# Two choices at once on four 64x64 quarters of the array, tile by tile, in a two-layer routed-expert kernel

## The reference, cut to what matters

```python
q = (xt @ w_query).reshape(n, 8, 2, 128)          # 16 units of 128 columns
s = einsum('nhpd,pkd->nhpk', q, subkeys)           # scores of 128 keys, twice a head
s1, i1 = top_k(s[:, :, 0], 16); s2, i2 = top_k(s[:, :, 1], 16)
best, ic = top_k(all sums s1 + s2, 16)             # 16 experts for each of 8 heads
expert, gate = i1[...] * 128 + i2[...], softmax(best)
act = gelu(einsum('nd,nhkd->nhk', xt, w_up[expert])) * gate
y = einsum('nhk,nhkd->nd', act, w_down[expert])    # 128 choices a token
```

## Time and profile before

| | before |
|---|---|
| device time, median of 3 runs (lowest, highest) | 5051.02 us (5049.02, 5064.87) |
| span of the profiled execution | 5042.8 us |
| PE matmul busy | 4367.6 us (87%) |
| DVE busy | 3163.9 us (63%) |
| ACT busy | 1188.3 us (24%) |
| POOL busy | 1621.6 us (32%) |
| moved by DMA | 1472.42 MB, mean 292 GB/s |
| choices' gathers (queue q0, with some other loads) | 1263.35 MB |

### The profile page before, as it was taken

How to read it: one execution, slowest core, us unless ns; L and a number is a source line. 1 busy time by engine, 2 the same in 40 slices (tenths; PEclk the granted TensorE clock), 3 DMA queues, 4 the chain that set the end, 5 groups by cost and what they waited for, 6 DMA issues and landing times. The chain is left out here.

```text
span 5042.8 us, 49934 instructions
## 1 busy us (share of the span) xinstructions
PE 4367.6 (87%) x17024; PEld 2583.3 (51%) x17024; DVE 3163.9 (63%) x7441; ACT 1188.3 (24%) x2971; POOL 1621.6 (32%) x1418
## 2 busy tenths in 40 slices
PE   8899999999989877789999897799999987777555
PEld 6866677755444323334476776776544443232111
DVE  6523323247878789855556644432778788995776
ACT  2211211113323323221111223110333232332111
POOL 0412000014444444433330241100444444444554
PEclk9999999999999999999999999999999999999777
DMA  2223232329999999999993234441999999999998
GB/s 110 84 74 120 73 127 96 137 115 415 415 409 410 416 420 413 412 420 419 419 419 149 84 109 166 169 163 40 387 419 404 412 413 420 420 413 418 416 414 342
DMA packets 266368, 1472.42 MB, mean 292 GB/s; under 512 B 27009, under 2 KB 77953, under 8 KB 113601
## 3 DMA queue, kind: packets, MB, share of 16 engines
q0 software_dynamic: 176608, 1263.35, 61.4%
q1 hardware_dynamic: 79168, 198.75, 10.7%
q10 hardware_dynamic: 10336, 7.12, 0.5%
HBM read 1433.90 MB, written 55.34 MB: 295 GB/s over the span
## 5 line engine op out<-in xcount | busy, mean ns | idle before, releaser
L3036 PE MATMUL ps<-early,diag 128*128 128x512 f32 (+1 forms) x3464 | 1692.2, 634 | 416.8 <-ACT diag L2944 416.3
L2826 POOL DMA_INDIRECT early<-in_peer,ids x980 | 1148.4, 1172 | 1430.1 <-PE ps L3036 1257.6
L2868 DVE SCALAR_TENSOR_TENSOR early<-early,rows 128x1024 f32<-128x1024 f32 x980 | 1184.2, 1223 | 443.9 <-DMA early<-in_peer,ids 441.8
L3036 PEld LDWEIGHTS ps<-early,diag 128*128 128x128 f32 (+1 forms) x3464 | 647.8, 195 | 1370.6 <-ACT diag L2944 679.0
L2944 ACT ACTIVATE diag<-consts_sb,weight 128x128 f32<-128x128 f32 (+1 forms) x1010 | 354.3, 391 | 769.5 <-DVE weight L2880 754.0
L1335 PE MATMUL ps<-hT,gate_ring 128*128 128x288 f32 (+2 forms) x1728 | 465.0, 424 | 6.4 <-ACT gate_out L1347 3.4
L1335 PEld LDWEIGHTS ps<-hT,gate_ring 128*128 128x128 f32 x1728 | 319.7, 193 | 144.9 <-issue 34.6
L2933 ACT ACTIVATE gel<-dot 128x2 f32<-128x2 f32 x576 | 117.4, 204 | 1116.3 <-DVE early L2868 925.0
L3036 PE MATMUL ps<-late,diag 128*128 128x512 f32 (+1 forms) x432 | 228.5, 671 | 83.5 <-ACT diag L2944 82.7
L2966 PE MATMUL ps<-late 128*128 128x320 f32 (+2 forms) x1024 | 251.8, 399 | 0.0
L2826 POOL DMA_INDIRECT late<-in_peer,ids x136 | 164.6, 1211 | 199.2 <-PE ps L3036 163.5
(11 more groups left out here) (394 smaller groups left out, 5859.3 us busy)
## 6 DMA issues: line engine op xcount, KB each, us to landing
gate_ring<-in_in_gate POOLq DMA_DIRECT2D x48, 512.0 KB, 4.2
slot<-in_w_branch SPq DMA_DIRECT2D x16, 1152.0 KB, 5.2
ring<-in_in_delta SPq DMA_DIRECT2D x8, 2048.0 KB, 8.4
late<-in_peer_query SPq DMA_DIRECT2D x32, 512.0 KB, 7.9
early<-in_peer,ids POOLq DMA_INDIRECT x980, 15.5
slot<-gate_rows SPq DMA_DIRECT2D x16, 864.0 KB, 7.0
slot<-in_in_pool SPq DMA_DIRECT2D x6, 2048.0 KB, 10.7
gate_ring<-in_in_gate SPq DMA_DIRECT2D x24, 512.0 KB, 10.8
```

What stands on the lines that cost most here:

```text
L2826: pool.indirect_dma_start(place(q), None, table_rows, bass.IndirectOffsetOnAxis(ap=ids[:, n, c:c + 1], axis=0)).then_inc(s.pair[PLACE[q]], 16)
L2868: nc.vector.scalar_tensor_tensor(out=up, in0=up, scalar=1.0, in1=rows[:, n, :], op0=ALU.mult, op1=ALU.mult, accum_out=dot[:, i % 2, k:k + ...
L3036: ins = nc.tensor.matmul(g.ps[0:r, 2 * (n % 2) + m, :], diag[:, (SUMMED[q] - 1) % DIAGS, 0:r], place(q)[:, D + m * 512:D + (m + 1) * 512], ...
```

## The change

All tiles go in turn. PE takes a group's two choices at once: the array is used as four quarters of 64 rows and 64 columns, for each half of the tokens (r) and each choice of the group (k). Choice k of half r is summed in PSUM partitions 64k to 64k+63, banks 2r and 2r+1. So a group is 8 matmul calls of 64x64 by 512 columns where it was 4 of 128x128. `x` is no longer added by PE nor copied by ACT: DVE adds the two choices' sums to it at the start of the next tile (`fold`), during which PE waits. DVE adds no choices of its own. Places come free by groups. Four more heads' halves are asked for ahead of group 0, the routes of tiles 0 and 1 are in one stretch of 60 groups, and the projections' units come one in each group, from group 209 on. The ring of 10 places ends at choice 32 and returns at choice 114.

```diff
-TOGETHER = 2
-HEADS = [(n, h) for h in range(PH) for n in range(TOGETHER)] + [(n, h) for n in range(TOGETHER, TILES) for h in range(PH)]
+HEADS = [(n, h) for n in range(TILES) for h in range(PH)]
+BY_GROUP = [(n, c) for n in range(TILES) for c in range(0, COUNT[n], GROUP)]
 ROUTE_AT = {}
 for _h in range(PH):
+    for _at, _head in ({0: (0, _h + 1), 4: (1, _h)} if _h < PH - 1 else {0: (1, _h)}).items():
+        ROUTE_AT.update({_h * STEP + _at + k: _head + (k,) for k in range(4)})
+for _i, _head in enumerate(itertools.product(range(2, TILES), range(PH), range(4))):
+    ROUTE_AT[PH * STEP + _i] = _head
...
-EXTENDED = 244
+EXTENDED = 114
-ASKED = ((0, 2), (3, 4), (6, 9), (11, 13))
+FIRST_ASKED = (("query", 0, 0), ("query", 1, 0), ("scores", 0, 0), ("scores", 1, 0), ("query", 0, 1), ("query", 2, 0), ("scores", 0, 1),
+               ("query", 1, 1), ("query", 3, 0), ("scores", 1, 1), ("scores", 2, 0), ("scores", 3, 0))
+REST_ASKED = {0: (("query", 2, 1),), 1: (("scores", 2, 1), ("query", 3, 1)), 2: (("scores", 3, 1),)}
+ASKED = {0: ("query", 0, 0), 1: ("query", 1, 0), 2: ("scores", 0, 0), 3: ("scores", 1, 0),
+         4: ("query", 0, 1), 5: ("query", 1, 1), 6: ("scores", 0, 1), 7: ("scores", 1, 1)}
+def asked_at(i):
+    step, at = divmod(i, STEP)
+    kind, v, a = ASKED[at]
+    return REST_ASKED.get(i, ()) + (((kind, 2 * (step + 2) + v, a),) if step + 2 < PH else ())
-BEGIN, BEGUN = (8, 9, 7, 0, 1, 2, 3, 4, 5, 6), 90
+BEGIN, BEGUN = (8, 9, 7, 0, 1, 2, 3, 4, 5, 6), 32
...
-    return [v for v in range(GATE_RUNS[RUN_AHEAD].total) if GATES_AT + 4 * v // 3 == i]
-BY_VECTOR = [q for q in range(2 * GATES_AT, PAIRS - 6) if q % 2 == 1]
+    return [v for v in range(GATE_RUNS[RUN_AHEAD].total) if GATES_AT + v == i]
+ORDER_OF_TILES = ((0, 0), (1, 1), (0, 1), (1, 0))
...
     def last_vector(self, dve, link):
-            nc.vector.tensor_copy(g.x[0:NS, LAST_TILE, a * 512:(a + 1) * 512], g.ps[0:NS, self.bank(a), :]).then_inc(s.x_half, 1)
+        dve.wait_ge(s.downs_done, len(BY_GROUP))
+        for a in range(2):
+            to = g.x[0:NS, LAST_TILE, a * 512:(a + 1) * 512]
+            link(nc.vector.tensor_tensor(to, to, g.ps[0:NS, a, :], ALU.add))
+            nc.vector.tensor_tensor(to, to, g.ps[NS:P, a, :], ALU.add).then_inc(s.x_half, 1)
...
+                    if LAST[q] >= 0:
+                        pool.wait_ge(s.downs_done, LAST[q] // GROUP + 1)
...
+            def fold(n):
+                dve.wait_ge(s.downs_done, TILE_END[n] + 1)
+                for r in range(2):
+                    rows_of_half = slice(r * NS, (r + 1) * NS)
+                    to = g.x[rows_of_half, n, :].rearrange("p (a c) -> p a c", a=2)
+                    link(nc.vector.tensor_tensor(to, to, g.ps[0:NS, 2 * r:2 * r + 2, :], ALU.add))
+                    nc.vector.tensor_tensor(to, to, g.ps[NS:P, 2 * r:2 * r + 2, :], ALU.add).then_inc(s.x_copied, 1)
...
-                if i:
-                    add_own(i - 1)
+                if c0 == 0 and n:
+                    fold(n - 1)
...
-                    nc.scalar.activation(diag[:, d % DIAGS, 0:ROWS[n]], table(g, "ident" if ROWS[n] == P else "ident2"), ACT.Copy,
+                    nc.scalar.activation(diag[:, q % DIAGS, :], table(g, "ident2"), ACT.Copy, scale=weight[:, i % 2, k:k + 1]
...
+            def sums(i, n, m):
+                for r, k in ORDER_OF_TILES:
+                    q, half = i * GROUP + k, slice(r * NS, (r + 1) * NS)
+                    last = nc.tensor.matmul(g.ps[k * NS:(k + 1) * NS, 2 * r + m, :], diag[half, q % DIAGS, :],
+                                            place(q)[half, D + m * 512:D + (m + 1) * 512], start=i == tile_group(n), stop=i == TILE_END[n])
+                return last
...
             for i, (n, c0) in enumerate(BY_GROUP):
-                if c0 == 0 and n != LAST_TILE - 1:
-                    add_x(n, True)
+                if c0 == 0 and n:
+                    pe.wait_ge(s.x_copied, 2 * n)
                 for kind, u, a in asking[i]:
+                    ask(kind, u, a)
                 following.tensor(pe, i)
+                pe.wait_ge(s.diagonal, (i + 1) * GROUP)
+                for m in range(2):
+                    last = sums(i, n, m) if n < LAST_TILE else sample_sums(i, n, m)
+                last.then_inc(s.downs_done, 1)
```

More of the change, by code:

```diff
@@ L2771, in score_expert_stage @@
     slots = ROUTE_AT
-    halves = [(u + v, a) for u in range(0, NQ, 2) for a in range(2) for v in range(2)]
+    asking = [asked_at(i) for i in range(len(BY_GROUP))]
+    halves = [(u, a) for part in [FIRST_ASKED] + asking for kind, u, a in part if kind == "query"]
     columns = lambda u, a: slice(NEAR, TOK) if a else slice(P if u < 2 else 0, NEAR)
     asked = lambda u, a: halves.index((u, a)) + 1
[L2775 to L2786, removed]
+    tile_group = lambda n: min(i for i, (m, c) in enumerate(BY_GROUP) if m == n)
     with nc.Block() as block:
@@ L2843, in first_route @@
                     route(0, 0, k)
[L2845 to L2852, removed]
-                        if q == FIRST_OWN:
-                            last = nc.vector.tensor_scalar(own[:], row, w, None, ALU.mult)
-                        else:
-                            to = own[:] if n == LAST_TILE else g.x[:, n, :]
-                            last = nc.vector.scalar_tensor_tensor(out=to, in0=row, scalar=w, in1=to, op0=ALU.mult, op1=ALU.add)
-                        last.then_inc(s.added, 1)
+            def fold(n):
[5 more added lines that the diff above has]
+                    nc.vector.tensor_tensor(to, to, g.ps[NS:P, 2 * r:2 * r + 2, :], ALU.add).then_inc(s.x_copied, 1)
             out.vector(dve, link, first_route)
@@ L2997, in scores, with ask, sample_sums @@
                 last.then_inc(s.far_sums if a else s.pe_b, 1)
-            def add_x(n, first):
-                r = ROWS[n]
-                for m in range(2):
-                    last = nc.tensor.matmul(g.ps[0:r, 2 * (n % 2) + m, :], ident(g, r), g.x[0:r, n, m * 512:(m + 1) * 512],
-                                            start=first, stop=not first)
+            def ask(kind, u, a):
+                if kind == "query":
+                    query(u, a)
+                else:
+                    scores(u, a)
+            def sums(i, n, m):
[4 more added lines that the diff above has]
+                return last
+            def sample_sums(i, n, m):
+                for k in range(GROUP):
+                    q = i * GROUP + k
+                    last = nc.tensor.matmul(g.ps[k * NS:(k + 1) * NS, m, :], diag[:, q % DIAGS, :],
+                                            place(q)[:, D + m * 512:D + (m + 1) * 512], start=i == tile_group(n), stop=i == TILE_END[n])
                 return last
```

125 lines of the change are left out of this document (32 added, 93 removed).

## The result

The kernel after takes 5122.95 us (median of 4 runs, 5118.58 to 5126.41), the kernel before on the same chip 5051.12 (4 runs, 5049.02 to 5064.87). The ratio is 1.0142, interval 1.0125 to 1.0159: 72 us slower, where 35 were forecast. The time lies inside the stated range, and the direction is the forecast's; the size is off by two. The profiled execution has a span of 5124.6 us, 81.8 above that of before. The two differences are not the same because executions vary: of one execution of the kernel after, the time and the span differ by 1.8 us, while the median of before stands 8.3 above its profiled span. So those 8.3 us are not a part that lies around the span, as the table of before has it; the profiled execution of before was some 6.5 us quicker than the median.

A forecast was written before the change was run, and what follows sets the result against it. DMA's gathers at about 420 GB/s were taken as the bound. First layer 10 + 17 - 1 = 26 us, second 10 - 1 = 9, together 35 on 5042.8, plus 8.2 to the median: 5086 us, range 5022 to 5145.

The forecast's parts named there:

- the units' 17 us: First layer, 54 groups from 209: PE 7.23 us a group against DMA's 6.73, 27 us less about 10 of slack.
- the 0 us of groups 16 to 64: Within groups 16 to 208: 8 groups take PE 34.3 us against DMA's 42.5, so PE is no bound and its dips go.
- The price of the sums: A group's sums on PE: four quarters abreast, 1.72 us, plus 0.35 us for switching to quarters and back.
- the two-abreast rival: A group's sums on PE run only two abreast, 3.43 + 0.35 us: 206 us slower, 5257 us; chance 0.15.
- the folds after tiles 2 and 3: The later two of a layer's four folds: they meet an idle DVE and cost nothing.
- dips under 415 GB/s: Sign against the forecast: such DMA rates between groups 8 and 56 would mean something else than PE's sums made them.
- The start: Each layer: queries ahead of the first sums delay the first places to about 1144 us, leaving DMA idle 20 us.
- The folds in groups 64 to 160: Two of four folds fall in DVE's dense groups 56 to 159: 7 us each less 10 of slack, about 4.5 a layer.
- The end: Each layer's last sums: 3.6 us less from column tiles and no `own`, some 2.6 given back by additions: minus 1 us.
- what the kernel before leaves idle up to group 208: DMA's idle time per layer before the change, taken as 14.5 us and set against 24.5 after: plus 10 us a layer.

The follow-up runs named there:

- experiment 1: Kernel after with the next layer's units again in three of four groups from 209 on: 5088.37 us, 34.6 less than after.
- experiment 3: Kernel after with each fold's four additions cut from 512 to 8 columns of each bank: 5111.49 us, 11.5 less than after.
- experiment 6: Kernel after with each unit's query and scores in turn, no two queries in a row: 5110.53 us, 12.4 less than after.
- experiment 7: Kernel after with seven places in place of eight from choice 32 to 113: 5162.79 us, 39.8 more than after.
- experiment 2: Kernel after with routes of tile 1 moved to groups 56 to 123, the others to as far as 187: 5127.16 us, no gain.
- experiment 5: Kernel after with each asked query's product cut to one matmul call of eight: 5091.66 us, 31.3 less than after.

## Why the direction was right and the size wrong

The mechanism of the largest term was right; the size failed in two steps, the units' 17 us and the 0 us of groups 16 to 64.

**The price of the sums** held: 1.72 + 0.35 = 2.07 us forecast; the period of 7.24 us is 7.23 as forecast, and the two-abreast rival is out. The strict order that the Trainium skill, "TensorE: Matmul & The Clock Gate", Part 3, states, and from which that rival came, is contradicted for such calls: by it the 16 records would have taken 3.43 us, and they took 1.95, or 1.97 with four in a row on one quarter.

**The units** are the step that failed most in one stretch. "Plus 17 us" was 27 less 10 of slack. The stretches have 28.2 more than before, and putting the units back (experiment 1) gave 30 us of stage and 35 of time. The excess is larger than 27: 36 units at 7.24 - 6.73 and 18 at 7.43 - 6.73 are 31.0, since the units of 128 columns take 5.62 us and not 5.43. To that comes the fold. The step said that the folds after tiles 2 and 3 "meet an idle DVE and cost nothing". DVE was idle, but the fold is a wait of PE, and the one after tile 3 lies where PE is the bound: 5.10 us of wait and 2.1 of a slower unit. That makes 38.2, of which some 6 us went into slack and 32 remain; the forecast had 10 and 17. Taking the fold's additions away gave 3.2 back (experiment 3). A cost had been asked of the engine that does the work and not of the one that waits for it.

**Groups 16 to 64** are the second failure, and over both layers the larger one: 18 us that were put at nothing, against the 11 by which the units were forecast too low. The forecast compared means, 34.3 us of PE work in a step of 8 groups against 42.5 of DMA, and let the dips go. I named dips under 415 GB/s as what would say that something else than PE's sums made them, and they came: 405. The means are right. But two groups with far queries in a row free places at 6.38 us each, against some 5.3 of DMA, and the places did not cover that. Order (experiment 6) and places (experiment 7) move this price; DVE's density (experiment 2) does not. Alternating took away less than half of it, so the rest stays open. Before, the ring of ten ended at choice 90, now at 32, so groups 16 to 45 have two places fewer; that this too is part of it was not tried, and the price of one place is a hint only. Nor was the clock: at 1354.95 sums took 3.69 us and not 1.95 while GpSimd had waited 7.38 us for a place.

**The start** came at the times forecast: first sums done at 1145.0 against 1144, the next 10.8 us later against 10.5. It was short by 24.1 us against 20. The forecast named the queries as its whole reason. By experiment 5 they are at least 11 us of it; the wait for the ring of query weights is part of what stands behind them. How much of the rest that wait makes, and how much the lower clock of that experiment, was not separated.

**The folds in groups 64 to 160**: 4.5 us a layer forecast, from two folds of 7 us and 10 of slack. The stretch is short by 9.4 and 8.2 us, 8.0 and 7.0 of them around the fold after tile 1; the one after tile 0 costs next to nothing. So the sum was near half of it and its split wrong. The dips of the kernel before did go, as forecast: the 315 us that had been short by 6.8 (411 GB/s) are short by 1.5. **The end** had -1 us a layer and got none: the last dot is 14.1 us ahead of the end, before 13.9. The last sums ran at the lower clock, 3.17 us and not the 1.72 forecast:

```profile
5112.85 3.17 PE L2990 MATMUL ps<-late,diag 128*64 128x512 f32 x8 [3.04 <-ACT diag L2921]
```

In sum, the first stage had 27 us forecast and 52 measured: start +4.1, groups 16 to 64 +9.0, 64 to 208 +5.5, from 208 on +11.2 (28.2 for 17), less 4.8, because the forecast took 14.5 us for what the kernel before leaves idle up to group 208 and the stretches show 6.3 + 2.4 + 10.6 = 19.3. The second had 10 forecast and 19 measured, for the first three reasons and without the units. Between the stages nothing was forecast and 9 were found; they are not explained.

## What to carry to other kernels

Faster sums on PE free nothing where DMA is the bound; what counts is the stretch with the least slack, and there one more unit for every three, planned because PE looked cheaper, made PE the bound and cost 30 to 35 us. Where work comes in bursts, compare the longest burst with what the ring of buffers covers, not the mean with the mean: the same work in alternating order gave 11 to 12 us. And ask of every new wait where the waiting engine is the bound, not only whether the engine waited for is free. Last, compare the same stretch, not only the whole time: 9 of the 39 us between the spans of after and of experiment 1 lay ahead of the edited code.

## What the hardware showed that I had not expected

PE keeps four quarters busy even when four consecutive records go to the same quarter: 1.97 us for a group's sums, against 1.95 with a new quarter in every call. That fits an engine that looks several records past the one that waits, though no row shows how far. And the mean granted clock fell from .957 to .878: with PE idle half the time in the middle of a stage, many of its sums ran at the 1.2 GHz level and not at 2.4 (3.69 us and not 1.95 in the row below, from after). In slices at 416 to 419 GB/s that cost nothing; what it cost where places were short was not measured.

```profile
1354.95 3.69 PE L2981 MATMUL ps<-early,diag 64*64 64x512 f32 x16 [5.76 <-ACT diag L2921]
```
